# 88 matmuls on zeros at the head of the local sink attention

## The reference

```python
def swa_gqa_sinks(q, k, v, sinks):          # 8 query heads, 2 key/value heads, 64 wide
    qc = q.reshape(b, nc, CHUNK, A_KV_HEADS, A_GROUP, HEAD_DIM)
    kb = chunk_band(k.reshape(b, nc, CHUNK, A_KV_HEADS, HEAD_DIM), A_BAND_CHUNKS)   # own chunk + 1
    vb = chunk_band(v.reshape(b, nc, CHUNK, A_KV_HEADS, HEAD_DIM), A_BAND_CHUNKS)
    scores = jnp.einsum('bnqkgd,bnskd->bnkgqs', qc, kb) * (HEAD_DIM ** -0.5)
    scores = jnp.where(valid[None, :, None, None, None, :], scores, NEG_INF)
    sink = sinks.reshape(1, 1, A_KV_HEADS, A_GROUP, 1, 1)
    m = jnp.maximum(jnp.max(scores, axis=-1, keepdims=True), sink)
    p = jnp.exp(scores - m)
    probs = p / (jnp.sum(p, axis=-1, keepdims=True) + jnp.exp(sink - m))
    return jnp.einsum('bnkgqs,bnskd->bnqkgd', probs, vb).reshape(b, s, A_Q_W)
```

## Time and profile before

| | |
|---|---|
| time, median of 3 runs | 3031.63 us (3024.8 to 3031.88) |
| profiled execution, its own time | 3054.76 us |
| profiled execution, span of the trace | 3053.3 us |
| mean granted TensorE clock over the span | 0.866 |
| stretch 1261 to 1480 us (local sink attention): TensorE busy | 170.73 us |
| the same stretch: VectorE, ScalarE, GpSimd busy | 83.70, 83.38, 69.48 us |
| the same stretch: granted clock | 0.50 |

### The profile page before, as it was taken

One profiled execution on the slowest core, in us unless ns is written; L12 is line 12 of the kernel. 1 busy time (PEld: TensorE's weight loads), 2 busy tenths in 40 slices (PEclk: granted clock), 3 DMA queues, 4 the chain that ended last, 5 costly groups with the idle time before them and its releaser, 6 DMA issues. The chain is left out here.

```text
span 3053.3 us, 40640 instructions
## 1 busy us (share of the span) xinstructions
PE 2597.7 (85%) x13149; PEld 2238.3 (73%) x13150; DVE 1391.9 (46%) x2350; ACT 1107.9 (36%) x1810; POOL 693.7 (23%) x650
## 2 busy tenths in 40 slices
PE   3999999999878888498499999762999999999950
PEld 2788888888668777498488888751888888888840
DVE  7100000000067777344432333122775768697858
ACT  4111111121155555353321212112564646576632
POOL 4000044441011010243010101004332323243342
PEclk6999999999978988555599999655999999999985
DMA  3121245442233333355533333333886768798868
GB/s 132 49 82 62 89 141 161 138 158 90 75 78 80 67 70 84 85 162 197 166 117 117 131 117 131 113 112 109 300 308 220 287 253 308 252 391 329 319 242 332
DMA packets 217200, 507.87 MB, mean 166 GB/s; under 512 B 53328, under 2 KB 70736, under 8 KB 212848
## 3 DMA queue, kind: packets, MB, share of 16 engines
q1 hardware_dynamic: 179440, 380.09, 37.1%
q0 software_dynamic: 26320, 85.56, 8.1%
q10 hardware_dynamic: 11376, 41.42, 3.5%
HBM read 390.03 MB, written 116.97 MB: 166 GB/s over the span
## 5 line engine op out<-in xcount | busy, mean ns | idle before, releaser
L327 DVE TENSOR_TENSOR pj_w_lo<-pj_w_raw,pj_w_hi 128x1024 fp32r<-128x1024 f32 x34 | 42.6, 1255 | 662.5 <-ACT pj_w_hi L266 662.3
L354 PE MATMUL pj_bank<-pj_hT_hi,pj_w_hi 128*128 128x512 f32 x1088 | 291.8, 390 | 3.5 <-DVE pj_w_lo L327 3.5
L354 PE MATMUL pj_bank<-pj_hT_lo,pj_w_hi 128*128 128x512 f32 x1088 | 291.6, 390 | 0.0
L354 PE MATMUL pj_bank<-pj_hT_hi,pj_w_lo 128*128 128x512 f32 x1088 | 291.1, 389 | 0.0
L354 PEld LDWEIGHTS pj_bank<-pj_hT_hi,pj_w_hi 128*128 128x128 f32 x1088 | 204.7, 188 | 46.3 <-issue 3.9
L354 PEld LDWEIGHTS pj_bank<-pj_hT_lo,pj_w_hi 128*128 128x128 f32 x1088 | 204.8, 188 | 42.6
L354 PEld LDWEIGHTS pj_bank<-pj_hT_hi,pj_w_lo 128*128 128x128 f32 x1088 | 204.7, 188 | 42.5
L1847 POOL TENSOR_TENSOR ex_wd_lo<-weights_raw_d,ex_wd_hi 128x1024 fp32r<-128x1024 f32 x64 | 194.4, 3058 | 131.5 <-ACT ex_wd_hi L1872 131.5
L1937 DVE TENSOR_TENSOR ex_wd_lo<-weights_raw_d,ex_wd_hi 128x1024 fp32r<-128x1024 f32 x64 | 169.1, 2681 | 9.8 <-ACT ex_wd_hi L1872 9.8
L802 PE MATMUL b_o_ps<-b_v_st,b_pt_hi 128*128 128x128 f32 x560 | 159.4, 315 | 10.2 <-DVE b_pt_lo L686 10.2
L277 ACT ACTIVATE pj_f_out<-pj_bank 128x512 f32<-128x512 f32 x72 | 37.2, 604 | 343.5 <-PE pj_bank L354 343.5
(11 more groups left out here) (242 smaller groups left out, 6351.2 us busy)
## 6 DMA issues: line engine op xcount, KB each, us to landing
weights_raw_g<-in_w_exp_gate_dram SPq DMA_DIRECT2D x128, 512.0 KB
weights_raw_u<-in_w_exp_up_dram SPq DMA_DIRECT2D x128, 512.0 KB
weights_raw_d<-in_w_exp_down_dram SPq DMA_DIRECT2D x128, 512.0 KB
scratch_ys<-ex_y ACTq DMA_DIRECT2D x47, 512.0 KB, 4.5
scratch_feat<-pj_f_out SPq DMA_DIRECT2D x36, 512.0 KB, 3.5
pj_w_raw<-in_w_feat_dram SPq DMA_DIRECT2D x34, 512.0 KB, 4.5
scratch_gates<-pj_f_out SPq DMA_DIRECT2D x32, 512.0 KB, 3.5
scratch_ys<-a_zeros POOLq DMA_DIRECT2D x32, 512.0 KB, 16.5
```

The source lines that it names most:

```text
L354: last = pe.matmul(eight[4 * p + b][:], w[p][:, k * P:(k + 1) * P], h[:, k, b * NB:(b + 1) * NB], start=(k == 0 and n == 0), stop=(k == KD ...
```

## The change

A tile `dense` of 128 x 512 is cleared by GpSimd as its first instruction. TensorE runs 40 matmuls of 128 x 512 with this tile as weights and as data as its first work in the stage, ahead of its waits for the loads, and 48 more between the turning of v and the first scores. They write to `o_ps[0]`, which the values of step 0 overwrite.

```diff
+DENSE = (40, 48)
...
+        dense = st.sb("dense", [P, NB], F32R)
...
+        dense_set = st.sem("dense_set")
...
         @block.gpsimd
         def _(pool):
+            pool.memset(dense[:].bitcast(F32), 0.0).then_inc(dense_set, 1)
             for g in range(2):
                 pool.memset(k_st[g][:, :CHUNK].bitcast(F32), 0.0).then_inc(padded, 1)
...
+            def run_dense(count):
+                for _ in range(count):
+                    pe.matmul(o_ps[0][:].rearrange("p n d -> p (n d)"), dense[:, :P], dense[:], start=True, stop=True)
+
+            pe.wait_ge(dense_set, 1)
+            run_dense(DENSE[0])
             pe.wait_ge(const_in, 32)
             pe.wait_ge(padded, 8)
             for b in range(V_BATCHES):
                 turn_v(0, b)
+            run_dense(DENSE[1])
             scores(0)
             scores(1)
             for u in range(A_STEPS):
```

## The result

The changed kernel took 3046.3 us (median of 6 runs, 3043.2 to 3051.6) against 3031.5 us for the kernel before (6 runs beside it): ratio 1.0049, 95% interval 1.0028 to 1.0070, so 8 to 21 us slower. Run again later beside other kernels, it came out at 1.0025 (1.0006 to 1.0044), 2 to 13 us. Slower both times, by 0.49% and 0.25%.

The account below looks back on a forecast made before the run. The prediction took TensorE at half clock to bound the local sink attention. The 48 matmuls add 9.3 us, the clock returns 1.2: +8.1 us on the median 3031.6 gives 3039.7 us, range 3029 to 3049.

Parts of the forecast that it names:

- the 0.54 us behind its upper bound: Burst of 48: cold matmul spacing taken from the chunked attention, weight load not hidden; 15.1 us, 11.9 on the path.
- What the clock gives back: Start-up behind the first scores: full clock wins 1.2 us until it falls about 6 us after them; 0.6 if by 3.4.
- The first gap: TensorE's start-up behind the first scores at full clock: gaps of 1.6 and 0.8 us, a pattern ahead of a clock fall.
- the early bound: Start-up: the clock falls by 3.4 us behind the first scores, so only 0.6 us is won.
- the 0.2 us for values that are still fast: Behind the second transposes: what little of the next values is still fast raises the gain from 1.0 to 1.2 us.
- It does not come back: Rest of the stage: after its fall the clock stays at 0.50, steps of 5.03 us as before.
- The rival in which the clock holds: First half of the stage at full clock, third pair 10 us earlier, clock falling there; 3022 us, chance 0.10.
- the third pair's wait: Third pair's scores wait 11.0 us for q_lo from GpSimd, behind its stores of zeros; wait expected to shift with early steps.
- The zeros: the rival: Bursts: matmuls on zeros do not raise the clock; 17.3 us on the path, nothing back, 3049 us, chance 0.04.
- the sum: Whole stage: +9.3 us of burst on the path less 1.2 us won gives +8.1, between +6.4 and +11.3.

Follow-up runs that it names:

- the placed: Against the kernel before: no burst ahead of the loads, 52 matmuls on zeros in the wait for v and 16 in that for q; ratio 0.9995.
- the filled: As "the placed", plus 7 matmuls on zeros after the scores of step 1 and 4 after those of step 2; ratio 0.9982 to the kernel before.
- the doubled kernel: The changed kernel with 96 matmuls on zeros in place of 48 between the turned v and the scores; ratio 1.0046 to the kernel before.
- the kernel with the copies of q later: "the filled" with GpSimd's zero stores after its last q split, ScalarE's copies one step later, 3 more matmuls on zeros in step 2; 0.9955 to the kernel before.
- zeros in every step: "the kernel with the copies of q later" plus 2 or 3 matmuls on zeros per step from step 2, zero stores by SyncE; 0.9808 to the kernel before.

## Why the prediction was right, point by point

**Direction and size.** Forecast 3039.7 us, range 3029 to 3049, slower 0.40 and same 0.49. Measured 3046.3, within the range, and slower by more than 0.3% in the first comparison, less in the second. The forecast for the stage was +8.1 us. Its traces with the 48 matmuls give 219.6, 219.8 and 219.4, those without 211.1, 210.9 and 211.9: means 219.6 and 211.3, +8.3. The total is less close: +14.8 us in the first comparison, +7.6 in the second, and 8.1 lies within the interval of the second (2 to 13) and just under that of the first (8.5 to 21). What bears the forecast out is the stage, not the 3046.3 us.

**The 40 matmuls: right.** Predicted 10.7 us, measured 11.15, and then the v batches at full clock. The kernel with these alone shows no effect on the time (0.9990), and at most about 1 us on the stage (211.9 against 211.1 and 210.9), which is gone at the next stage's first matmul (226.4 and 226.4).

**The 48 matmuls: right.** Predicted 12.5 us, measured 12.36. Six of them came before the clock rose, and not eight; those behind it followed each other after 0.227 us, and the first took 0.59. The scores start 9.9 us later, predicted 9.3; the rest is that the third v batch came 27.3 us after the stage's start and not 26.4. It comes at 27.2 in the kernel with the first 40 only, and at 26.2 with the memset only and with the last 48 only, so these 0.9 us go with the first burst. The traces show by what way. ScalarE turns to v only after q, and its wait for q's load ends 21.5 to 21.6 us after the stage's start in the four kernels with the first burst, and after 20.4 to 20.8 in the ten without. Why the load lands later beside the burst stays open. The reason that the prediction gave for the 0.54 us behind its upper bound, a weight load that is not hidden, is not shown either: in the trace that load ended 0.10 us before its matmul started.

**What the clock gives back: right.** The first transposes 3.5 us behind the scores (predicted 3.5), the second 5.9 (5.9). The first gap is 1.60 us, predicted 1.6; the second is 0.1 and not 0.8, since the clock had fallen before it and the scores ahead of it took longer. The fall came at 4.0 us, predicted about 6 with 3.4 as the early bound. Returned: 9.9 - 8.5 = 1.4 us, predicted 1.2. That these two are so close is in part luck, for two terms were off and offset each other. Before the change the second transposes start 7.29 us behind the first score at 1296.74, and not 6.9:

```profile
1304.03 1.12 PE L1157 MATMUL a_pt_ps<-a_idt,a_prob 128*128 128x128 f32 x4
```

They waited for ScalarE's exponentials, which end at 1303.97, and not only for the next scores. So 1.36 us were won up to there, and not 1.0; and the 0.2 us for values that are still fast came to nothing, since the clock was down before they began.

**It does not come back: right.** In the placed, the filled and the doubled kernel it never rose again in the stage either, through long stretches in which TensorE was busy without a pause.

**The rival in which the clock holds: refuted for the change, and too small as a prize.** The rule on idle gaps in the Trainium skill ("TensorE: Matmul & The Clock Gate", "Why this matters for your kernels": "No PE-idle gaps >~3µs between matmul bursts") does not carry this far: the clock fell with no gap above 1.6 us in the changed kernel, and beside a pause of 1.2 us in the kernel with the copies later. Where gaps were filled, it held as long as they were. The working of the rival also stopped at the first pair's steps: it did not see the late q load, which the kernel with filled gaps ran into at step 2. And I took the third pair's wait as given; with the stores moved and zeros in every step the clock held through, and the stage was 59 us shorter than at half clock (140.4 against 199.6).

**The zeros: the rival fell.** The clock rose on matmuls whose operands are all zero, in each of the ten kernels that had them, 2.6 to 4.9 us after the first of them.

**What the sum left out.** The first comparison gave +14.8 us and the stage +8.5, or +9.0 to the next stage's first matmul, which is inside the interval of 8 to 21. The kernels without the burst and the repeat show no second cost of the edit. The stages told of below, which no edit touched, differ by more than these 6 us from one execution to the next. That the difference is theirs is likely but not shown, since only one execution of each kernel was traced.

## What to carry to other kernels

A burst that raises TensorE's clock is free only in a wait that is there anyway, and is worth only what the work right behind it keeps: see first whether that work, at the higher clock, would leave TensorE waiting, for then the clock is gone within a few microseconds (here 3.7 to 5.0 us behind the first scores, in the five kernels with a burst ahead of them and the gaps left open). If the work is too thin, spread the filler over its steps (here two matmuls of 0.22 us in each step of 3.1) rather than put it ahead; and expect each gap you close to uncover the next, a load or a copy that was never late at half clock. Check the size of a change of a few tenths of a per cent in the trace, not in the total, and measure there to the first work of the next stage: the stage's last instruction does not show a transfer that ends late.

## What the runs showed of the hardware that was not expected

**The same stage at different clocks.** The chunked attention, which no edit touched, took 416 us in the trace of before, and in the traces of the other kernels 438, 436, 423, 431, 436, 417, 438, 439, 423, 438, 433, 423 and 430. It alternates between the two levels of the clock, and where it falls differs from execution to execution. Two stretches that hold it, before and in the changed kernel, with a clock of 0.81 and 0.74:

```profile
809.00:1261.00 452.00, 366.10 (x2354) 334.08 (x2352) 308.20 (x838) 231.45 (x479) 45.74 (x36) 0.81 0.31 71
```

```profile
809.00:1284.00 475.00, 394.39 (x2357) 363.68 (x2355) 309.77 (x838) 231.75 (x480) 45.82 (x36) 0.74 0.30 69
```

The routing stage did the opposite: 159 us at 0.50 in the trace of before, and 122 us at a mean of 0.68 in all the others, changed or not. So two traces can differ by 20 to 40 us in stages that an edit never touched, and a comparison of whole spans (3053.3 before, 3050.0 after) had even the sign wrong.

**VectorE beside GpSimd.** In the kernel with the copies later a VectorE instruction on 128x4 elements took 1.28 and 1.30 us while GpSimd ran its subtraction of q, and it stood in the chain of these steps, which came to 3.2 us. Of the 32 such instructions of the stage, the 21 that no subtraction of GpSimd's overlaps took 0.23 us. Of the 11 that one overlaps, four took 0.99 to 1.30 us and seven 0.23. So the long instructions all stand beside GpSimd, but not all that stand there are long; what decides it was not tried.

```profile
1337.39 1.28 DVE L1083 TENSOR_SCALAR a_neg<-a_top,a_nsink 128x4 f32<-128x4 f32 x1
1340.63 1.30 DVE L1083 TENSOR_SCALAR a_neg<-a_top,a_nsink 128x4 f32<-128x4 f32 x1
```
